# Routing joined, high and low parts gathered apart, expert weights with eight neighbouring features per partition

## The chip, the cores and the metric

The kernel runs on one core of one Trainium2 chip, alone. The metric is the device time of one execution in microseconds. TensorE (PE), VectorE (DVE), ScalarE (ACT), GpSimd (POOL) and SyncE (SP) run side by side, each through its own list of instructions, and wait for each other by semaphores.

## What is computed

Two layers of a decoder trunk on 256 tokens of 1024 features, all in float32. A layer is a mixer of three kinds of attention, a cross-attention into 256 memory tokens, and a grouped mixture of experts, each followed by a layer norm. The change is in the third part, `TOP_K` is 2, with four groups of four experts:

```python
scores = jax.nn.sigmoid(x @ router_w)                  # 16 experts
biased = scores + router_bias
grp = biased.reshape(B, S, 4, 4)
g_sel = jnp.argmax(jnp.sum(lax.top_k(grp, 2)[0], axis=-1), axis=-1)
masked = jnp.where(in_group[..., None], grp, NEG_INF).reshape(B, S, 16)
_, expert_idx = lax.top_k(masked, 2)
w = jnp.take_along_axis(scores, expert_idx, axis=-1)
w = w / jnp.sum(w, axis=-1, keepdims=True)             # gates of the two
a = jax.nn.silu(x @ w_gate[e]) * (x @ w_up[e]) * gate[e]
out = sum over e of a @ w_down[e]                      # x <- LayerNorm(alpha*x + out)
```

## The kernel before, in words

**Products in two parts.** Every large product runs in fp32r, with each operand split in a high and a low part. `product` (lines 1467 to 1471) makes three matmuls, high by high, high by low, low by high. ScalarE writes the high part of a weight (`split_hi`, a rounding copy), VectorE the low one (`split_lo`, a subtraction).

**The weight stream.** Weights come in sub-loads of up to 512 KB, in a fixed order, through a ring of 12 slots (`raw`). SP issues the load of sub i when the low part of sub i − 12 is made. There are four slots for split weights; ScalarE splits sub i when TensorE has used sub i − 4. N1 is the number of the first sub of the experts. An expert takes four subs for gate and up (each two chunks of 128 features, 256 gate columns and 256 up columns) and two for down.

**The order of the mixture part, in a layer.** Each engine's order is written out by hand.
- `x` is transposed to `xT`, features on partitions, in a high and a low part. TensorE forms the router product "RT" with the weights as the stationary side, 16 experts (and unused columns) by 256 tokens. ScalarE copies it to `logitT`, TensorE turns it back to tokens on partitions ("GT", lines 1851 to 1858), and ScalarE takes the exponential.
- VectorE works out the group of each token (`router_groups`, 1148 to 1177), step by step, each waiting for the one before. `first_best` marks the first maximum in a row, one operation per tile of 128 tokens. The group comes out as `ing`, a 0/1 table.
- Meanwhile ScalarE makes `xs_hi`, the high part of `x`, and GpSimd `xs_lo` (659 to 662).
- TensorE counts each token's place in its group with products by the tables `upto` and `ones` in fp32 (1677 to 1684), VectorE turns this to `posg` and to `sel`, a 0/1 table of tokens by 4 × 128 places.
- `gather`: for each of 8 chunks f of 128 features, four matmuls (high and low part, two tiles) add up in one bank of PSUM the features f*128 to f*128+127 of the tokens of all groups. ScalarE and VectorE copy the banks in turn to `xg`, in float32.
- For each group the token block is split to `cur_hi` and `cur_lo` (`cur_of`, lines 768 to 771 and 1231 to 1236), for group 0 at once, for the others between the splits of the group before, at its second expert.
- Experts in turn: `experts_up` (24 matmuls of 512 columns), `act_of`, `turn_a`, `experts_down` (12). `turn_sel` comes between the first two experts, `place_gates` in the middle of the second expert's up part. `router_first` and `router_gates` (1190 to 1223) work out the two experts and their gates; the end of `router_gates` finds whether a group has over 128 tokens and sets `flag`.
- `y_of` reads a group's result, `scatter` puts it back to the tokens.

## Time and profile before

| | us |
|---|---|
| median of 3 runs | 956.23 |
| the runs | 952.37, 956.23, 956.77 |
| the profiled execution | 951.58 |
| its span, first to last instruction | 950.0 |
| TensorE busy (matmul) | 835.7 (88%) |
| VectorE busy | 648.5 (68%) |
| ScalarE busy | 496.9 (52%) |
| GpSimd busy | 95.0 (10%) |

The span is the time between the first and last instruction, the rest of the profiled execution lies around it. Busy times are sums over the span; matmuls overlap, so two that follow each other at once show starts closer together than their durations. A matmul has two rows, its load of the stationary operand (PEld, LDWEIGHTS) and itself (PE, MATMUL). In the timeline, instructions of one line that follow each other are merged in one row ("x2"), and the bracket names the idle time of that engine before the row and who ended it. The mean granted TensorE clock is 0.946 of full.

### The profile page before, as it was taken

What the parts mean: (1) busy time and instruction counts of PE and PEld (TensorE: products, weight loads), DVE (VectorE), ACT (ScalarE), POOL (GpSimd) and SP (SyncE); (2) the same over time, 40 slices, a digit from 0 to 9 for tenths busy, and PEclk for the clock granted to TensorE, in tenths of its full rate; (3) what the DMA queues carried; (4) which work ended last, traced back from release to release, by engine and by line L of the source; (5) the groups of instructions that cost most, each with busy time, mean ns of one, the idle gap of its engine ahead of it and who ended that gap; (6) DMA issues with size and microseconds to landing.
All of it is one profiled execution on the core that took longest, in us unless ns stands there. A gap on an engine that the chain in (4) does not pass through costs nothing.

```text
span 950.0 us, 12092 instructions
## 1 busy us (share of the span) xinstructions
PE 835.7 (88%) x4292; PEld 701.7 (74%) x4292; DVE 648.5 (68%) x1137; ACT 496.9 (52%) x799; POOL 95.0 (10%) x169
## 2 busy tenths in 40 slices
PE   4989999989965899999689989999898489999994
PEld 4987887879854677777488878878886467777773
DVE  6456766574547798989555576577564667989983
ACT  4555544444333587877345554454443335878761
POOL 7122200020012000000121130002000200000001
PEclk9999999999977999999989999999999589999997
DMA  9842432653322599999364425344524227999931
GB/s 305 270 134 98 156 123 94 218 179 112 114 86 89 170 333 350 337 346 338 103 181 132 145 90 178 111 159 158 171 92 134 83 73 262 346 344 351 339 108 45
DMA packets 124094, 177.06 MB, mean 186 GB/s; under 512 B 12304, under 2 KB 92704, under 8 KB 124032
## 3 DMA queue, kind: packets, MB, share of 16 engines
q1 hardware_dynamic: 122048, 169.56, 53.7%
q0 software_dynamic: 1984, 6.70, 2.3%
q8 instruction: 36, 0.59, 0.3%
q14 instruction: 26, 0.21, 0.1%
HBM read 175.18 MB, written 1.05 MB: 186 GB/s over the span
## 4 chain that ended last, share of the span: by engine, by line
PE 75%; DVE 14%; ACT 4%; issue 3%; POOL 2%; ACTq 0%; DVEq 0%; POOLq 0%
PE bank L1469 20%; PE bank L1471 19%; PE bank L1470 19%; DVE w_lo L515 5%; PE bank L1692 2%; ACT w_hi L509 2%; PE bank L1619 2%; PE bank L1723 2%; PE bank L1599 2%; PE bank L1588 1%; PE bank L1577 1%; PE bank L1628 1%; PE bank L1566 1%; DVE xT_lo L1004 1%; PE bank L1576 1%
## 5 line engine op out<-in xcount | busy, mean ns | idle before, releaser
L515 DVE TENSOR_TENSOR w_lo<-raw,w_hi 128x1024 fp32r<-128x1024 f32 (+2 forms) x336 | 382.4, 1174 | 87.2 <-ACT w_hi L509 86.1
L509 ACT ACTIVATE w_hi<-raw 128x1024 fp32r<-128x1024 f32 (+2 forms) x336 | 326.2, 1007 | 121.7 <-PE bank L1471 121.1
L1469 PE MATMUL bank<-w_hi,cur_hi 128*128 128x512 f32 x256 | 104.5, 408 | 8.5 <-DVE w_lo L515 8.5
L1471 PE MATMUL bank<-w_hi,cur_lo 128*128 128x512 f32 x256 | 101.3, 396 | 0.0
L1470 PE MATMUL bank<-w_lo,cur_hi 128*128 128x512 f32 x256 | 101.0, 395 | 0.0
L1469 PE MATMUL bank<-w_hi,xT_hi 128*128 128x384 f32 (+1 forms) x224 | 79.2, 353 | 8.3 <-DVE xT_lo L1004 7.9
L1470 PE MATMUL bank<-w_lo,xT_hi 128*128 128x384 f32 (+1 forms) x224 | 76.8, 343 | 0.0
L1471 PE MATMUL bank<-w_hi,xT_lo 128*128 128x384 f32 (+1 forms) x224 | 76.7, 342 | 0.0
L614 POOL TENSOR_SCALAR st<-st 128x1 f32<-128x1 f32 x12 | 7.0, 581 | 678.2 <-ACT junk L760 677.7
L718 ACT ACTIVATE qkT<-bank 66x512 f32<-66x512 f32 (+2 forms) x32 | 19.0, 594 | 90.3 <-PE bank L1566 90.3
L1469 PEld LDWEIGHTS bank<-w_hi,cur_hi 128*128 128x128 f32 x256 | 48.7, 190 | 21.2 <-DVE w_lo L515 6.7
L1469 PE MATMUL bank<-w_hi,aT_hi 128*128 128x512 f32 x128 | 53.0, 414 | 8.3 <-DVE w_lo L515 6.0
L1471 PEld LDWEIGHTS bank<-w_hi,cur_lo 128*128 128x128 f32 x256 | 48.7, 190 | 10.6
L1470 PEld LDWEIGHTS bank<-w_lo,cur_hi 128*128 128x128 f32 x256 | 48.9, 191 | 9.1
L1469 PE MATMUL bank<-xT_hi,w_hi 128*128 128x256 f32 x144 | 45.3, 315 | 9.1 <-DVE xT_lo L1004 9.1
L1469 PE MATMUL bank<-w_hi,mixT_hi 128*128 128x512 f32 x128 | 51.0, 398 | 0.0
L1469 PEld LDWEIGHTS bank<-w_hi,xT_hi 128*128 128x128 f32 x224 | 43.0, 192 | 10.7 <-issue 9.2
L1471 PE MATMUL bank<-w_hi,aT_lo 128*128 128x512 f32 x128 | 50.8, 397 | 0.0
L1470 PE MATMUL bank<-w_lo,aT_hi 128*128 128x512 f32 x128 | 50.7, 396 | 0.0
L1470 PE MATMUL bank<-w_lo,mixT_hi 128*128 128x512 f32 x128 | 49.9, 390 | 0.0
L1471 PE MATMUL bank<-w_hi,mixT_lo 128*128 128x512 f32 x128 | 49.9, 390 | 0.0
L775 ACT ACTIVATE aT_hi<-bank 128x256 fp32r<-128x256 f32 x32 | 12.3, 384 | 63.3 <-PE bank L1648 63.3
(291 smaller groups left out, 1684.1 us busy)
## 6 DMA issues: line engine op xcount, KB each, us to landing
raw<-in_expert_w_gate_dram SPq DMA_DIRECT2D x128, 256.0 KB, 4.3
raw<-in_expert_w_up_dram SPq DMA_DIRECT2D x128, 256.0 KB, 5.0
raw<-in_expert_w_down_dram SPq DMA_DIRECT2D x64, 512.0 KB, 4.9
raw<-in_w_in_dram SPq DMA_DIRECT2D x48, 384.0 KB, 4.1
raw<-in_xattn_w_kv_dram SPq DMA_DIRECT2D x32, 512.0 KB, 3.5
raw<-in_w_mix_out_dram SPq DMA_DIRECT2D x16, 512.0 KB, 4.2
raw<-in_xattn_w_q_dram SPq DMA_DIRECT2D x16, 512.0 KB, 4.3
raw<-in_xattn_w_o_dram SPq DMA_DIRECT2D x16, 512.0 KB, 4.3
```

The costliest lines, as they stand in the source:

```text
L509: nc.scalar.activation(w_hi[:, split_slot(i, p), 0:w], raw[:, slot, 0:w], ACT.Copy).then_inc(hi_ready.sem, 1)
L515: nc.vector.tensor_tensor(w_lo[:, split_slot(i, p), 0:w], raw[:, slot, 0:w], w_hi[:, split_slot(i, p), 0:w].bitcast(F32), ALU.subtract).th ...
L718: nc.scalar.activation(qkT[0:d, h % 2, :], B_QK[0:d, :], ACT.Copy).then_inc(qkT_ready.sem, 1)
L775: nc.scalar.activation(aT_hi[:, par, :, :], bank[2 + par][:, 0:2 * P].rearrange("p (c t) -> p c t", c=2), ACT.Copy).then_inc(aT_a.sem, 1)
L1004: nc.vector.tensor_tensor(xT_lo[:, 4 * h:4 * h + 4, t * P:(t + 1) * P], b[:, :].rearrange("p (k m) -> p k m", k=4), hi.bitcast(F32), ALU.s ...
L1469: nc.tensor.matmul(o, lhs[0], rhs[0], start=first, stop=False, skip_group_check=shared)
L1470: nc.tensor.matmul(o, lhs[0], rhs[1], start=False, stop=False, skip_group_check=shared)
L1471: return nc.tensor.matmul(o, lhs[1], rhs[0], start=False, stop=last, skip_group_check=shared)
L1599: ins = nc.tensor.transpose(B_PT[:, k * P:(k + 1) * P], pr[:, k * P:(k + 1) * P], ident[:, :])
L1619: nc.tensor.matmul(o[:, 0:T], v[:, 0, g, :], pT[:, h % 2, 0:T], start=True, stop=False)
L1692: ins = nc.tensor.matmul(bank[XG_BANK[f]][:, :], v[:, t, f * P:(f + 1) * P], sel[:, t, :], start=n == 0, stop=n == 3)
L1723: ins = nc.tensor.matmul(bank[2 * t + h][:, :], selT[:, g, t * P:(t + 1) * P], v[:, g, 512 * h:512 * h + 512], start=g == 0 and v is y_hi, ...
```

## The change

Router: the product is turned over, the tokens are the stationary side and 16 expert columns are moved, so the logits come out with tokens on partitions. Routing works on both tiles in one operation each, with broadcast operands; the score of a group, the sum of its two largest, is found as the maximum of three kinds of pairs; the two experts of a token come from counting how many of the four in its group are ahead. `upto`, `ones` and `ing` become fp32r, and `xs_lo` is made by VectorE. The gather keeps the high and the low part in banks of their own and writes them as `xg_hi` and `xg_lo`, so `cur_of` is gone. Its stationary operand takes every eighth column, so partition p of chunk f holds feature 8p + f; the gate and up weights are read by the same rule, so that a sub brings rows 8p+2j and 8p+2j+1 to partition p. `full_group` is split off `router_gates` and comes after the first `act_of`. At the start of the kernel VectorE writes `ones`, `upto` and `earlier`, and TensorE waits for them. The tables `desc16` and `logitT` are gone; places in SBUF are moved.

```diff
+        XG_BANKS = ((6, 7), (2, 3), (0, 1))
+        LO_BY_ACT = (2, 5)
+        spread = lambda w: w.rearrange("(p k) n -> p k n", p=P)
...
-                    load(l, i + j, slot, [(r[:, :, g, :], feat(w[l][e])[:, 2 * j:2 * j + 2, :])
+                    load(l, i + j, slot, [(r[:, :, g, :], spread(w[l][e])[:, 2 * j:2 * j + 2, :])
                                           for g, w in enumerate((expert_w_gate, expert_w_up))])
...
-                for t in range(TT):
-                    pool.wait_ge(xs_a.sem, xs_a.at(l, t + 1))
-                    nc.gpsimd.tensor_tensor(xs_lo[:, t, :], xs[:, t, :], xs_hi[:, t, :].bitcast(F32), ALU.subtract)\
-                        .then_inc(xs_p.sem, 1)
...
-                wait_job(l, "RT")
-                nc.scalar.activation(logitT[0:NE, :], bank[2 * pair["RT"]][0:NE, 0:T], ACT.Copy).then_inc(job_a.sem, 1)
-                wait_job(l, "GT")
-                nc.scalar.activation(rt[:, 0, :], bank[2 * pair["GT"]][:, 0:TT * NE], ACT.Exp, scale=-1.0)\
                 for t in range(TT):
                     nc.scalar.activation(xs_hi[:, t, :], xs[:, t, :], ACT.Copy).then_inc(xs_a.sem, 1)
+                wait_job(l, "RT")
+                nc.scalar.activation(rt[:, 0, :], banks("RT")[0][:, 0:TT * NE], ACT.Exp, scale=-1.0)\
+                    .then_inc(job_a.sem, 1)
...
-                for f in range(0, KC, 2):
+                for f in range(KC):
                     act.wait_ge(xg_done.sem, xg_done.at(l, f + 1))
+                    for n, dst in ((0, xg_hi), (1, xg_lo)):
+                        if n == 0 or f in LO_BY_ACT:
+                            nc.scalar.activation(dst[:, f, :, :].rearrange("p g s -> p (g s)"),
+                                                 bank[XG_BANKS[f % 3][n]][:, :], ACT.Copy).then_inc(xg_a.sem, 1)
...
+            nc.vector.tensor_copy(ones[:, :], ones_f[:, :]).then_inc(fp_tables, 1)
+            nc.vector.tensor_copy(upto[:, :], upto_f[:, :]).then_inc(fp_tables, 1)
+            nc.vector.tensor_scalar(earlier[:, :, :], order[:, :, :], 0.5, None, ALU.is_gt).then_inc(fp_tables, 1)
...
+                step(nc.vector.tensor_scalar(R[1], R[0], 1.0, None, ALU.add))
+                step(nc.vector.reciprocal(R[2], R[1]))
+                step(nc.vector.tensor_tensor(by_tile(R[3], NE), by_tile(R[2], NE),
+                                             rbias[:, :].unsqueeze(1).to_broadcast([P, TT, NE]), ALU.add))
+                step(nc.vector.tensor_tensor(more, first, second, ALU.max))
+                step(nc.vector.tensor_tensor(both, first, second, ALU.add))
+                step(nc.vector.tensor_tensor(across, more[:, :, 0], more[:, :, 1], ALU.add))
+                step(nc.vector.tensor_tensor(within, both[:, :, 0], both[:, :, 1], ALU.max))
+                step(nc.vector.tensor_tensor(score, across, within, ALU.max))
+                step(nc.vector.tensor_reduce(best, by_tile(score, NG), AX, ALU.max))
+                step(nc.vector.tensor_tensor(cand, by_tile(score, NG), best.unsqueeze(2).to_broadcast([P, TT, NG]), ALU.is_equal))
+                step(nc.vector.tensor_tensor(G4(R[10]), G4(R[10]), desc4[:, :], ALU.mult))
+                step(nc.vector.tensor_reduce(ahead, cand, AX, ALU.max))
+                step(nc.vector.tensor_tensor(by_tile(ing_r[:, :], NG), cand, ahead.unsqueeze(2).to_broadcast([P, TT, NG]), ALU.is_equal))
...
...
...
                 turn_x(l, "XT1c", 1)
+                for t in range(TT):
+                    dve.wait_ge(xs_a.sem, xs_a.at(l, t + 1))
+                    nc.vector.tensor_tensor(xs_lo[:, t, :], xs[:, t, :], xs_hi[:, t, :].bitcast(F32), ALU.subtract)\
+                        .then_inc(xs_v.sem, 1)
                 for i in range(N1, N1 + 2):
                     split_lo(dve, l, i)
+                router_groups(l)
+                split_lo(dve, l, N1 + 2)
+                place_tokens(l)
+                for f in range(KC):
+                    if f not in LO_BY_ACT:
+                        dve.wait_ge(xg_done.sem, xg_done.at(l, f + 1))
+                        nc.vector.tensor_copy(xg_lo[:, f, :, :].rearrange("p g s -> p (g s)"),
+                                              bank[XG_BANKS[f % 3][1]][:, :]).then_inc(xg_v.sem, 1)
+                    if f == 1:
+                        split_lo(dve, l, N1 + 3)
+                    if f == 4:
+                        router_first(l)
                 split_lo(dve, l, N1 + 4)
-                router_gates(l, step)
                 split_lo(dve, l, N1 + 5)
+                router_gates(l)
                 dve.wait_ge(gs_done.sem, gs_done.at(l, 1))
...
                 act_of(l, 0, 0)
+                full_group(l)
                 for i in range(N1 + 6, N1 + 8):
...
-                        if j == 1:
-                            for h in range(2):
-                                cur_of(l, p + 1, h)
...
+            pe.wait_ge(fp_tables, 3)
             pe.wait_ge(mem_in, 16)
...
-                        lhs = tuple(v[:, kc, :] for v in (cur_hi, cur_lo))
+                        lhs = tuple(v[:, kc, e // EPG, :] for v in (xg_hi, xg_lo))
...
+                    for n, v in enumerate((xs_hi, xs_lo)):
+                        for t in range(TT):
+                            ins = nc.tensor.matmul(bank[XG_BANKS[f % 3][n]][:, :], v[:, t, f:DM:KC], sel[:, t, :],
+                                                   start=t == 0, stop=t == TT - 1)
...
+                routers = [sub_in(l, index["RT", j]) for j in range(2)]
                 for t in range(TT):
+                    for kc in range(KC):
+                        lhs = tuple(v[:, kc, t * P:(t + 1) * P] for v in xT)
+                        r = tuple(v[:, (kc % 4) * NE:(kc % 4 + 1) * NE] for v in routers[kc // 4])
+                        ins = product(banks("RT")[0][:, t * NE:(t + 1) * NE], lhs, r, t == 0 and kc == 0,
+                                      t == TT - 1 and kc == KC - 1, shared=True)
+                ins.then_inc(split_free.sem, 2)
                 gather(l)
-                experts_up(l, N1, 0, range(4), None, 0)
+                experts_up(l, 0, N1, range(4))
                 turn_sel(l)
```

## Rows read from the trace of the kernel before

**Rows 1.** The page, section 4: the chain by engine.
```profile
PE 75%; DVE 14%; ACT 4%; issue 3%; POOL 2%; ACTq 0%; DVEq 0%; POOLq 0%
```

**Rows 2.** Windows of layer 0: length, busy us (instructions), granted clock, DMA share, GB/s.
```profile
340.00:354.00 14.00, 13.40 (x59) 10.15 (x58) 12.49 (x15) 11.16 (x15) 0.00 (x0) 1.00 1.02 343
...
285.00:297.70 12.70, 2.27 (x10) 2.21 (x10) 9.42 (x25) 5.44 (x7) 5.78 (x4) 0.60 0.23 83
...
312.00:326.00 14.00, 10.56 (x51) 8.42 (x50) 9.52 (x24) 6.58 (x9) 0.00 (x0) 0.88 0.43 139
```

**Rows 3.** Timeline, product and routing: start us, duration us, instruction [idle <-releaser].
```profile
278.54 0.55 PE L1469 MATMUL bank<-xT_hi,w_hi 128*128 128x256 f32 x1 [2.27 <-DVE xT_lo L1004]
...
283.59 0.41 PE L1471 MATMUL bank<-xT_hi,w_lo 128*128 128x256 f32 x1
...
284.97 0.20 ACT L894 ACTIVATE rt<-bank 128x32 f32<-128x32 f32 x1 [0.56 <-PE bank L1855]
...
285.20 0.18 DVE L1158 TENSOR_SCALAR rt<-rt 128x32 f32<-128x32 f32 x1 [4.71 <-ACT rt L894]
...
285.42 0.35 DVE L1159 RECIPROCAL rt<-rt 128x32 f32<-128x32 f32 x1
...
286.19 4.67 POOL L661 TENSOR_TENSOR xs_lo<-xs,xs_hi 128x1024 fp32r<-128x1024 f32 x2 [14.06 <-ACT xs_hi L898]
...
286.22 2.34 DVE L1165 TENSOR_TENSOR rt<-rt 128x8 f32<-128x8 f32 x1
...
288.56 2.33 DVE L1167 TENSOR_TENSOR rt<-rt 128x8 f32<-128x8 f32 x1
...
292.69 0.16 DVE L1143 TENSOR_REDUCE rt<-rt 128x2 f32<-128x8 f32 x1
...
292.89 0.49 DVE L1145 TENSOR_SCALAR ing<-rt 128x4 f32<-128x4 f32 x2
```

**Rows 4.** Timeline, ranking, gather and the first expert, TensorE.
```profile
293.53 0.56 PE L1679 MATMUL bank<-ing,upto 128*128 128x4 f32 x2 [8.59 <-DVE ing L1145]
...
293.95 0.57 PE L1679 MATMUL bank<-ing,ones 128*128 128x4 f32 x2
...
297.75 0.77 PE L1692 MATMUL bank<-sel,xs_hi 128*128 128x512 f32 x1 [1.95 <-DVE sel L1184]
...
306.74 0.39 PE L1469 MATMUL bank<-w_hi,cur_hi 128*128 128x512 f32 x1
```

**Rows 5.** Loads of TensorE: two source lines (ns min/median/max) and a timeline row.
```profile
L1679 PEld LDWEIGHTS bank<-ing,upto x8: 288/333/338, 293.5 to 759.5; 128*128 128x128 f32 x8
...
L1692 PEld LDWEIGHTS bank<-sel,xs_hi x32: 187/188/338, 297.7 to 772.2; 128*128 128x128 f32 x32
...
317.84 1.98 PEld L1701 LDWEIGHTS bank<-g,sel 128*128 128x128 f32 x16
```

**Rows 6.** Timeline, first expert.
```profile
310.59 0.18 DVE L1203 SCALAR_TENSOR_TENSOR rt<-rt 128x32 f32<-128x32 f32 x1
...
315.31 1.21 DVE L515 TENSOR_TENSOR w_lo<-raw,w_hi 128x1024 fp32r<-128x1024 f32 x1
...
316.57 0.51 PE L1469 MATMUL bank<-w_hi,cur_hi 128*128 128x512 f32 x1 [1.96 <-DVE w_lo L515]
```

**Rows 7.** Timeline, `cur_lo` beside expert 2.
```profile
344.44 1.29 DVE L1235 TENSOR_TENSOR cur_lo<-xg,cur_hi 128x512 fp32r<-128x512 f32 x2
...
347.06 0.47 PE L1469 MATMUL bank<-w_hi,cur_hi 128*128 128x512 f32 x1 [0.55 <-DVE w_lo L515]
```

**Rows 8.** The page, section 6: pieces, KB each, us to landing.
```profile
raw<-in_expert_w_gate_dram SPq DMA_DIRECT2D x128, 256.0 KB, 4.3
...
raw<-in_xattn_w_kv_dram SPq DMA_DIRECT2D x32, 512.0 KB, 3.5
```

**Rows 9.** Timeline, start of the kernel.
```profile
8.29 3.32 PE L1460 MATMUL bank<-ident,mem_tok 128*128 128x128 f32 x16 [8.29 <-POOL offf L571]
...
8.35 1.08 DVE L986 TENSOR_SCALAR offs<-offs 128x256 int32<-128x256 int32 x2 [0.99 <-DMA rbias<-in_router_bias_dram]
```

More of the change, by code:

```diff
@@ L225, in build @@
         qTx, e4 = sb("qTx", [P, KC, T], at=q_work)
-        xg, m0 = sb("xg", [P, KC, NG, P], at=work)
-        cur_hi, m1 = sb("cur_hi", [P, KC, P], F32R, at=m0)
-        cur_lo, m2 = sb("cur_lo", [P, KC, P], F32R, at=m1)
+        xg_hi, m0 = sb("xg_hi", [P, KC, NG, P], F32R, at=work)
+        xg_lo, m2 = sb("xg_lo", [P, KC, NG, P], F32R, at=m0)
         y_hi, m3 = sb("y_hi", [P, NG, DM], F32R, at=m2)
@@ L1155, in step, with router_groups @@
                     dve.wait_ge(route.sem, route.at(l, q[0]))
[L1157 removed]
+                return step
+            def router_groups(l):
+                q[0] = 0
+                step = stepper(l)
+                dve.wait_ge(job_a.sem, job_a.at(l, evac_a[job["RT"]]))
                 step(nc.vector.tensor_scalar(R[1], R[0], 1.0, None, ALU.add))
                 step(nc.vector.reciprocal(R[2], R[1]))
[L1160 to L1162 removed]
@@ new lines, in router_groups @@
+                four = R[3].rearrange("p (g i) -> p g i", i=EPG)
+                first, second = four[:, :, 0:EPG:2], four[:, :, 1:EPG:2]
+                more, both = (R[i][:, 0:2 * TT * NG].rearrange("p (g i) -> p g i", i=2) for i in (4, 5))
+                step(nc.vector.tensor_tensor(more, first, second, ALU.max))
+                step(nc.vector.tensor_tensor(both, first, second, ALU.add))
+                across, within, score = (G4(R[i]) for i in (6, 7, 8))
+                step(nc.vector.tensor_tensor(across, more[:, :, 0], more[:, :, 1], ALU.add))
@@ L1430, in _ @@
                         expert_turn(l, p * EPG + (j + 1), (j + 1) % 2, 6 * j, p, p if j == EPG - 1 else None)
-                        if j == 1:
-                            for h in range(2):
-                                cur_of(l, p + 1, h)
                 for j in range(2):
@@ L1786, in _ @@
                     for s in range(t + 1):
-                        ins = nc.tensor.matmul(o, (ones if s < t else upto)[:, :], lf[:, s, :], start=s == 0, stop=s == t)
+                        ins = nc.tensor.matmul(o, (ones if s < t else upto)[:, :].bitcast(F32), lf[:, s, :],
+                                               start=s == 0, stop=s == t)
                 ins.then_inc(turned.sem, 1)
```

231 lines of the change are left out of this document (88 added, 143 removed), and 2 rows, old and new, of the table jobs.

## The prediction

> **What bounds the kernel now.** I read the chain that ended last first: 75% of it lies on TensorE, 14% on VectorE [rows 1]. So a microsecond counts only where TensorE waits, or where its own list of work gets longer or shorter. Then I read stretches of layer 0 [rows 2]. In the expert stage (340 to 354) TensorE is busy 13.40 of 14 us at the full clock, 59 matmuls or 0.23 us each, with the DMA engines at 1.02 and 343 GB/s. In the routing stretch (285 to 297.7) it is busy 2.27 of 12.70 us while VectorE is busy 9.42: there VectorE is the path, and there this change works. All of it happens twice; layer 1 repeats the pattern.
>
> The reader should see three things in the timeline. First, the last product matmul starts at 283.59, the first routing step at 285.20, and the last half of `ing` is written at about 293.4, so routing takes 8.2 us. In it two operations of 8 columns take 2.34 and 2.33 us, where their like take 0.16, just while GpSimd forms `xs_lo` (4.67 us for two) [rows 3]. Second, ranking, `sel` and gather follow one another, up to the first expert at 306.74 [rows 4]. Third, TensorE waits 1.96 us for a weight split that stands in VectorE's queue behind `router_gates` [rows 6].
>
> **The change, part by part, per layer.** Durations are of the one profiled execution.
>
> *Router product: a cost.* Now 24 matmuls move 256 columns each; from 278.54 to 283.59 are 23 intervals of 0.22 [rows 3], the low of TensorE's two levels (256 columns at 1.2 GHz are 0.21). After it there are 3 × 8 × 2 = 48 matmuls that move 16 columns, each with its own load of 128 columns, and the load is the price. The trace has no fp32r matmul of so few columns. The nearest rows: the ranking's fp32 passes of 4 columns, two of which begin 0.42 after the two before, 0.21 each at the low level [rows 4]; and the 16 loads of `place_gates` in 1.98, 0.12 each, at the high one [rows 5]. A load takes the same in both types (fp32 0.333 at the low level, the slowest fp32r one 0.338) [rows 5], so I take the same interval. The stretch begins after a wait of 2.27 and keeps the low level to its end [rows 3]. I take 48 × 0.213 = 10.2 against 5.1: +5.1. Bounds: +0.6, if it has the full clock at once (48 × 0.12 = 5.7), and +15, if a small fp32r matmul needs two passes as an fp32 one does (48 × 0.42 = 20).
>
> *Hop to routing: a gain.* The copy of `logitT`, the two transposes and their waits go. From the product's end (283.59 + 0.41) to 285.20 are 1.2; Exp (0.20) and two hand-overs stay, 0.3. −0.9 [rows 3].
>
> *Group routing: the gain.* `xs_lo` goes to VectorE, ahead of routing: two operations of about 1.2 like a weight split (1.21 [rows 6]), beside the product, which has its inputs already and is now 10 us long; the splits of N1 and N1+1 queue behind them (2.4), and on these only loads 12 sub-loads ahead wait. GpSimd then does nothing beside routing, so 2.34 and 2.33 become 0.2 each. The chain is 13 steps: 12 × 0.20, since a small step starts 0.20 after the one before (292.69, 292.89), and a reciprocal, 0.39 with its hand-over: 2.8 against 8.2. −5.4 [rows 3]. If another stall came in the place of GpSimd's, 4.3 of this would stay. What could be late next is split N1+2, queued between routing and `place_tokens` (1.2): ScalarE has its high half some 2.5 after Exp (function table, Silu, split), and VectorE would wait 1.3 for the ranking there anyway. I cost it at nothing, at 1.2 if that cover fails.
>
> *Ranking: a gain.* Five products in fp32 are ten passes, in fp32r five: −5 × 0.21 = −1.1 [rows 4]; 0 if fp32r of 4 columns takes two passes.
>
> *Gather: nothing, with a wide bound.* 32 matmuls before and after, 8.99 from the first to the expert's first, 0.28 each, partly at the low level [rows 4]. Their loads now take every eighth column. The trace has no such load; contiguous ones take 0.187 [rows 5] and can follow each other every 0.12. The moving side (512 columns, 0.23 at the high level [rows 2]) sets the pace, so there is no gain below nothing, and only a load of over 0.23 shows. No row bounds that above; I choose four times 0.12: 32 × (0.48 − 0.23) = +8. I take 0, since even twice the contiguous time hides. Ten evacuations on ScalarE and six plus a split on VectorE fit in some 8 us, with three pairs of banks in turn; as they write the high and low parts at once, `cur_hi` and `cur_lo` of group 0 go too.
>
> The Trainium skill speaks against this part. Its page "SBUF — State Buffer" (section "Door 1: The DMA port swizzle") says that reads want two hits in a line of 16 bytes and that each crossing to a new line pays a penalty; a step of eight fp32 columns has one hit per line. It gives no size for TensorE, and no row here shows one. By the rule the load gets longer, by how much is rival B.
>
> *First expert: a gain.* `router_gates` (from 310.59) stands before split N1+5 (315.31), and TensorE idles 1.96 [rows 6]. After the change the split comes first, ready about 5 us after the expert begins (two subs of 1.36 freed, ScalarE 1.0, VectorE 1.2); TensorE needs it after 24 × 0.23 and eight transposes, 6.5. The wait goes; the nine steps of `router_gates` (2) end before TensorE asks for `g4`. But `full_group` (four steps, 0.8) now stands behind `act_of` and ahead of split N1+6, for which TensorE waits already. −2.0 + 0.8 = −1.2.
>
> *Later groups: a gain.* `cur_lo` (two operations, 1.29) stands between splits and TensorE waits 0.55 behind it [rows 7], three times a layer. −1.6. The stalls behind `y_of` are not touched.
>
> *Weight loads: nothing.* Pieces stay 1 KB at the destination, 256 KB land in 4.3 us, and a slot comes round only after 12 sub-loads, some 17 us, so about 10 us of lateness is covered. Rows with a pitch of 8 KB are read already, `w_kv`, 512 KB in 3.5 [rows 8].
>
> *Start: a cost, once.* TensorE now also waits for three small VectorE operations behind `offs2`, which starts at 8.35 and takes 1.08; with 0.5 for the three TensorE begins at 10.0, not 8.29 [rows 9], and the way to the first product goes through these transposes. +1.7, between 0 (something later hides it) and 3.
>
> Sum per layer: 5.1 − 0.9 − 5.4 − 1.1 + 0 − 1.2 − 1.6 = −5.1; twice, and the start: −10.2 + 1.7 = −8.5. Against the profiled execution, 951.58 with a span of 950.0, that is 943.1. The median of the three runs is 4.65 above the profiled one; from it, 956.23 − 8.5 = 947.7. I forecast 947.5.
>
> **Rivals.** (A) The product gets the full clock, or its loads are cheaper than the fp32 rows say: +0.6 instead of +5.1, 9 less in all, 938.5. For it: it is twice as long and never pauses. Against it: 16 moved columns per load leave the array mostly idle, and in the stretch that holds `place_gates`, of the same kind, the granted clock is 0.88 over 312 to 326 although TensorE is busy for 10.56 of 14 [rows 2].
> (B) Slower: the strided load binds the gather. From 0.23 a load on every further 0.1 costs 3.2 per layer; from 0.36 on it eats the whole gain, and at 0.48 it is 16 for both: 963.5. This is what the skill's rule would do here. For it speaks only that no row shows a strided load; against it, that a contiguous load leaves half of the interval free.
> (C) Small fp32r matmuls need two passes: product +15, not +5, ranking no gain: 947.5 + 2 × 11 = 969.5.
> (D) The change does not do what it says: another stall, or split N1+2, keeps routing slow, 4 a layer: 955.5, no change.
>
> **How the numbers follow.** The forecast with its own small errors (±4) 0.55, A 0.18, B 0.12, C 0.05, D 0.10. Within 0.5% of 956.23, about what a measurement of this kernel can tell from no change, lies 951.4 to 961.0. Faster: A and nearly all of the forecast, 0.70. Slower: C and the upper end of B, 0.10. The rest of B, D and the forecast's upper end are no change, 0.20. The range leaves out C and the ends of A and B: 938 to 960.
>
> **What would show it.** Routing near 2.8 with no step over 0.4 in it; 48 loads 0.21 apart in the product (0.12 says A, 0.42 says C); loads of the gather near 0.19 (over 0.23 says B); no idle of 1.96 before the second expert, some 1.5 before its third sub; no idle of 0.55 in later groups; the first transpose at 10. The prediction is wrong if the product's loads have another price, or if loads set the pace of the gather.

## The result, and the profile after

The changed kernel takes 943.6 us (median of four runs, 942.97 to 944.69), the kernel before 956.48 on the same chip (952.37 to 956.77). The ratio is 0.988, 95% interval 0.985 to 0.991: faster, by 1.2%. The forecast was 947.5 in a range of 938 to 960. The two profiled executions are closer together, 951.58 and 944.16: 7.4 us, where 8.5 were worked out.

The chain of the page, by engine; before it was 75% and 14% [rows 1].

```profile
PE 82%; DVE 9%; ACT 3%; issue 3%; POOL 2%; DMA 1%; DVEq 0%; ACTq 0%; POOLq 0%
```

VectorE's share is 5 points smaller, TensorE's 7 larger: the routing became short, the router product long. The windows of layer 0 say the same (length, busy us with instructions in the order PE, PEld, DVE, ACT, POOL, granted clock, DMA share, GB/s).

```profile
273.00:282.00 9.00, 3.93 (x16) 3.13 (x16) 6.72 (x8) 4.01 (x8) 3.75 (x6) 0.51 0.22 73
282.00:292.60 10.60, 10.32 (x48) 10.31 (x48) 4.63 (x4) 1.02 (x2) 0.00 (x0) 0.50 0.45 137
292.60:299.00 6.40, 1.39 (x7) 1.28 (x6) 5.25 (x18) 3.58 (x5) 0.00 (x0) 0.50 0.15 44
299.00:304.00 5.00, 5.00 (x12) 4.03 (x13) 1.99 (x3) 1.19 (x2) 0.00 (x0) 0.51 0.12 50
304.00:309.00 5.00, 5.00 (x22) 4.96 (x22) 3.31 (x8) 3.75 (x7) 0.00 (x0) 1.00 0.30 105
```

The second row is the product: TensorE is busy for 10.32 of 10.60 us and the granted clock is 0.50, the lower level, throughout. It stays there until about 304, deep in the gather. GpSimd does nothing from 282 on.

The timeline of the same stretch answers to [rows 3, 4].

```profile
282.27 0.35 PE L1466 MATMUL bank<-w_hi,xT_hi 128*128 128x16 f32 x1 [2.27 <-DVE xT_lo L1001]
...
292.29 0.36 PE L1468 MATMUL bank<-w_hi,xT_lo 128*128 128x16 f32 x1
...
292.69 0.20 ACT L898 ACTIVATE rt<-bank 128x32 f32<-128x32 f32 x1 [9.67 <-PE bank L1468]
...
292.92 0.18 DVE L1153 TENSOR_SCALAR rt<-rt 128x32 f32<-128x32 f32 x1 [6.18 <-ACT rt L898]
...
295.56 0.17 DVE L1173 TENSOR_TENSOR ing<-rt 128x8 fp32r<-128x8 f32 x1
295.76 1.22 DVE L528 TENSOR_TENSOR w_lo<-raw,w_hi 128x1024 fp32r<-128x1024 f32 x1
...
295.78 0.37 PE L1677 MATMUL bank<-ing,upto 128*128 128x4 f32 x1 [3.13 <-DVE ing L1173]
...
298.89 1.21 PE L1691 MATMUL bank<-sel,xs_hi 128*128 128x512 f32 x2 [1.88 <-DVE sel L1183]
...
308.94 0.39 PE L1466 MATMUL bank<-w_hi,xg_hi 128*128 128x512 f32 x1
```

The 48 small matmuls start from 282.27 to 292.29, (292.29 − 282.27) / 47 = 0.213 apart, 10.2 us in all. Routing runs from 292.92 to 295.73, 2.8 us, with no step over 0.35. The gather takes 308.94 − 298.89 = 10.05 us, 8.99 before.

In the first expert, against [rows 6], the wait of 1.96 is gone. The over-full test (its last step at 321.29) stands ahead of the split that TensorE waits for:

```profile
320.78 0.53 PE L1647 MATMUL bank<-ident,act_a 128*128 128x128 f32 x2 [0.85 <-DVE act_a L1227]
...
321.29 0.16 DVE L1222 CAST flag<-fl 1x2 int32<-1x2 f32 x1
321.37 2.34 DVE L528 TENSOR_TENSOR w_lo<-raw,w_hi 128x1024 fp32r<-128x1024 f32 x2
...
322.63 0.79 PE L1466 MATMUL bank<-w_hi,xg_hi 128*128 128x512 f32 x1 [1.32 <-DVE w_lo L528]
```

At the start TensorE waits for the last of the three new conversions, and begins at 9.99 in place of 8.29 [rows 9]:

```profile
9.99 1.30 PE L1457 MATMUL bank<-ident,mem_tok 128*128 128x128 f32 x5 [9.99 <-DVE earlier L983]
```

The two spans are 950.0 and 942.4 us. Where the difference lies, from the starts of the rows that bound each stretch (us, after less before):

| stretch | layer 0 | layer 1 | worked out |
|---|---|---|---|
| start to the product of layer 0 | +3.73 | | +1.7 |
| end of layer 0 to the product of layer 1 | | −1.03 | 0 |
| product's start to the ranking | −1.48 | −1.16 | −1.2 |
| ranking to gather | −1.11 | −1.31 | −1.1 |
| gather | +1.06 | +0.17 | 0 |
| first expert to the transposes of the fifth | −1.27 | −1.09 | −1.7 |
| from there to the scatter | −1.32 | −2.82 | −1.1 |

The stretch from the scatter of layer 1 to the end is 20.8 us before and 20.9 after. The rows add up to −7.63, against −8.5 worked out. Two of them are in part chance of the two executions. In the last one of layer 1, 1.5 of the 2.82 lie in the down product of the last expert, 4.36 us before and 2.85 after: over 926 to 930 the granted clock of the kernel before was 0.59, while in the changed kernel it was 1.00 at this place (918 to 922). In layer 0 neither kernel has such a stretch there. The first, +3.73, is taken up again below.

### The profile page after: what moved, and what is told of

Same layout as the page of the kernel before. It is cut to its first block, busy times and chain, and to the rows that moved or that the text cites. A ratio compares the mean times of both kernels' runs of the same rounds, so it can differ in the third digit from the quotient of the medians.

```text
span 942.4 us, 12097 instructions
## 1 busy us (share of the span) xinstructions
PE 845.8 (90%) x4326; PEld 714.4 (76%) x4326; DVE 629.4 (67%) x1090; ACT 494.6 (52%) x793; POOL 85.6 (9%) x165
## 4 chain that ended last, share of the span: by engine, by line
PE 82%; DVE 9%; ACT 3%; issue 3%; POOL 2%; DMA 1%; DVEq 0%; ACTq 0%; POOLq 0%
PE bank L1466 22%; PE bank L1468 21%; PE bank L1467 21%; DVE w_lo L528 3%; PE bank L1691 2%; PE bank L1616 2%; PE bank L1720 2%; PE bank L1596 2%; PE bank L1585 2%; PE bank L1574 1%; PE bank L1625 1%; PE bank L1563 1%; DVE xT_lo L1001 1%; PE bank L1573 1%; ACT w_hi L522 1%
## 5 line engine op out<-in xcount | busy, mean ns | idle before, releaser
L1466 PE MATMUL bank<-w_hi,xg_hi 128*128 128x512 f32 x256 | 105.2, 411 | 2.7 <-DVE w_lo L528 2.7
L1468 PE MATMUL bank<-w_hi,xg_lo 128*128 128x512 f32 x256 | 102.0, 399 | 0.0
L1467 PE MATMUL bank<-w_lo,xg_hi 128*128 128x512 f32 x256 | 102.0, 399 | 0.0
L1466 PE MATMUL bank<-w_hi,xT_hi 128*128 128x384 f32 (+2 forms) x256 | 90.7, 354 | 12.1 <-DVE xT_lo L1001 11.7
L1468 PE MATMUL bank<-w_hi,xT_lo 128*128 128x384 f32 (+2 forms) x256 | 88.4, 345 | 0.0
L1467 PE MATMUL bank<-w_lo,xT_hi 128*128 128x384 f32 (+2 forms) x256 | 88.4, 345 | 0.0
L1468 PEld LDWEIGHTS bank<-w_hi,xg_lo 128*128 128x128 f32 x256 | 49.2, 192 | 11.3
L1467 PEld LDWEIGHTS bank<-w_lo,xg_hi 128*128 128x128 f32 x256 | 49.4, 193 | 9.2
L1467 PEld LDWEIGHTS bank<-w_lo,xT_hi 128*128 128x128 f32 x256 | 53.7, 210 | 0.3
L1468 PEld LDWEIGHTS bank<-w_hi,xT_lo 128*128 128x128 f32 x256 | 53.6, 209 | 0.2
```

The source lines that it names most:

```text
L1466: nc.tensor.matmul(o, lhs[0], rhs[0], start=first, stop=False, skip_group_check=shared)
L1467: nc.tensor.matmul(o, lhs[0], rhs[1], start=False, stop=False, skip_group_check=shared)
L1468: return nc.tensor.matmul(o, lhs[1], rhs[0], start=False, stop=last, skip_group_check=shared)
```

## The experiments

Each run is compared with the kernel before on its own chip; where it is set against the changed kernel, that is the first of the table. e0 to e2b ran on one chip, e3 to e6 on a second, e7 to e9 on a third, e10 on a fourth. The medians of the kernel before were 953.83, 954.61, 953.00 and 953.52 there, so a difference of about 1 us between runs of different chips says nothing by itself.

| kernel | median us | ratio to before | interval |
|---|---|---|---|
| e0_after | 944.03 | 0.990 | 0.988 to 0.993 |
| e1_product_back | 934.29 | 0.981 | 0.978 to 0.983 |
| e2a_pool_early | 944.70 | 0.992 | 0.989 to 0.994 |
| e2b_pool_late | 952.08 | 0.998 | 0.996 to 1.000 |
| e3_contiguous | 943.65 | 0.989 | 0.986 to 0.993 |
| e4_one_cur | 947.00 | 0.992 | 0.990 to 0.995 |
| e5_casts_late | 942.72 | 0.988 | 0.984 to 0.991 |
| e6_full_later | 943.49 | 0.989 | 0.986 to 0.993 |
| e7_all | 931.55 | 0.978 | 0.973 to 0.982 |
| e8_filled | 937.05 | 0.984 | 0.980 to 0.988 |
| e9_all_filled | 920.26 | 0.965 | 0.961 to 0.969 |
| e10_more_filled | 917.25 | 0.961 | 0.958 to 0.964 |

### The changed kernel again

> The changed kernel once more, beside the three variants below on the same chip, so that differences of a few us can be read. Every theory expects 943 to 945 us (its first runs: 943.0 to 944.7), and in the trace the router product of layer 0 in 48 matmuls 0.21 us apart and 10.2 us long.

944.03 us (943.08 to 944.49), the product from 282.36 to 292.38. The kernel before had a median of 953.83 here. So the change is worth 10 to 13 us by medians (9.8 here, 12.9 in the first comparison).

### The router product alone in its old form

```
-  routers = [sub_in(l, index["RT", j]) for j in range(2)]
-  for t in range(TT): for kc in range(KC): ...   # tokens stationary, 16 columns moved
+  lhs = tuple(v[:, k * NE:k * NE + P] for v in parts)
+  ins = product(banks("RT")[0][:, 0:T], lhs, tuple(v[:, kc, :] for v in xT), ...)
...
+  nc.tensor.transpose(banks("GT")[0][:, t * NE:(t + 1) * NE], logitT[0:NE, t * P:(t + 1) * P], ...)
```

> The changed kernel with the router product alone put back in its old form: 24 matmuls of 256 columns, the copy of the logits, the two small transposes and a third hop before the exponential. Theory of the prediction (the new product is 5.1 us a layer dearer than the old one at the low clock, the hop that goes with it 0.9 cheaper): this kernel is 4.2 us a layer faster than the changed kernel, 8.4 together, 935 to 936 us. Theory that the small matmuls also keep the granted clock low for longer (in the changed kernel it returns at 303.9 us, during the gather; in the kernel before it returned at 301.3): the gather is faster too, by up to 1.5 us a layer, and the whole 932 to 934 us. Rival: xs_lo and the split of the routers' weights stand on VectorE beside the product, so a shorter product only waits for them: less than 3 us gained in all, 941 us or more, and the trace then shows TensorE idle behind VectorE ahead of the ranking matmuls.

934.29 us: 9.7 faster than the changed kernel. Its timeline of layer 0:

```profile
280.65 0.55 PE L1469 MATMUL bank<-xT_hi,w_hi 128*128 128x256 f32 x1 [2.27 <-DVE xT_lo L1004]
...
285.70 0.35 PE L1471 MATMUL bank<-xT_hi,w_lo 128*128 128x256 f32 x1
...
290.19 0.34 PE L1680 MATMUL bank<-ing,upto 128*128 128x4 f32 x1 [3.22 <-DVE ing L1176]
...
293.27 1.22 PE L1694 MATMUL bank<-sel,xs_hi 128*128 128x512 f32 x2 [1.88 <-DVE sel L1186]
...
303.84 0.40 PE L1469 MATMUL bank<-w_hi,xg_hi 128*128 128x512 f32 x1
```

From the product's start to the ranking are 9.54 us, with the straight product 295.78 − 282.27 = 13.51: 4.0 less, the −4.2 of the theory. In layer 1 it is 13.51 against 9.61, 3.9, and the gather there is 9.15 in place of 10.35, since the clock is back sooner (at about 753.5, 3 us after the gather's start; in the changed kernel at about 764.5, over 5 us after it). In layer 0 the gather is no shorter: 10.57 in place of 10.05, with the granted clock at 0.50 over its first 6 us. The rival fell, nothing stood behind VectorE. The first theory holds for 7.9 of the 9.7 us. The second came true in one layer of two, and its gain is not steady. The profiled executions differ by 10.7 us, of which 1.6 lie ahead of the product of layer 0, where the two kernels are the same. So the part of the change that does away with the turning back is a loss of about 8 us, hidden under the gain of the others.

One number of this timeline is worth a look: 24 matmuls of 256 moved columns begin (285.70 − 280.65) / 23 = 0.220 apart, the first interval being long and the others 0.21, and those of 16 columns 0.213 apart. **At the lower level a matmul of 16 columns costs TensorE as much as one of 256.**

### What made the routing short: the place of `xs_lo`, or its engine

In e2a_pool_early, GpSimd forms `xs_lo` again, at the new early time; in e2b_pool_late moreover ScalarE makes `xs_hi` behind the exponential, as before the change.

```
-  dve: nc.vector.tensor_tensor(xs_lo[:, t, :], xs[:, t, :], xs_hi[:, t, :].bitcast(F32), ALU.subtract)
+  pool: nc.gpsimd.tensor_tensor(xs_lo[:, t, :], xs[:, t, :], xs_hi[:, t, :].bitcast(F32), ALU.subtract)
e2b only: the two copies to xs_hi moved from ahead of wait_job(l, "RT") to behind the exponential
```

> The changed kernel with xs_lo computed on GpSimd again (two subtractions of 4.7 us), but begun at the new early place of xs_hi, so that it runs beside the router product and ends before or with the routing's first steps. Theory (the saving in the routing came from where this work stands in time, beside the product, and not from the engine that does it): within 1.5 us of the changed kernel, 942 to 946 us. Since the second subtraction ends about 292 us after the start, at most the routing's first step should be touched. Rival (it is the engine: GpSimd's subtraction and VectorE's work beside it slow each other wherever they meet): the splits of the routers' weights on VectorE are late, the product starts later, and the whole is 4 us or more slower, 948 us or more.

> The changed kernel with xs_hi copied after the exponential, as before the change, and xs_lo on GpSimd behind it, beside the new routing of 13 steps. Theory (before the change two waits of 2.3 us stood in the routing because VectorE had to wait while GpSimd subtracted; they are worth 4.3 us a layer and come back with the overlap): 8 to 9 us slower than the changed kernel, 951 to 953 us, with two routing steps of over 2 us in the trace in place of 0.2 us. Rival (the steps themselves were what the old routing cost, the overlap was incidental): the 13 steps stay at 0.2 us each, the only cost is that xs_lo is later for the gather, and the whole is within 3 us of the changed kernel.

e2a 944.70 us, the same as the changed kernel; e2b 952.08, 8.1 slower. The rows of e2a, GpSimd and the VectorE split beside it:

```profile
280.34 6.55 POOL L674 TENSOR_TENSOR xs_lo<-xs,xs_hi 128x1024 fp32r<-128x1024 f32 x2 [6.28 <-ACT xs_hi L900]
...
280.07 4.56 DVE L528 TENSOR_TENSOR w_lo<-raw,w_hi 128x1024 fp32r<-128x1024 f32 x2
```

And of e2b:

```profile
294.69 4.67 POOL L674 TENSOR_TENSOR xs_lo<-xs,xs_hi 128x1024 fp32r<-128x1024 f32 x2 [18.03 <-ACT xs_hi L904]
...
294.74 2.34 DVE L1167 TENSOR_TENSOR rt<-rt 128x16 f32<-128x16 f32 x1
297.11 2.27 DVE L1169 TENSOR_TENSOR rt<-rt 128x8 f32<-128x8 f32 x1
```

Where two long operations meet, both are slowed: two splits take 4.56 in place of 2.35, GpSimd 6.55 in place of 4.67. Where GpSimd meets the small steps, it takes 4.67 as before the change, and two steps are held: an operation of 16 columns takes 2.34 and one of 8 columns 2.27, in place of 0.17. In e2a the meeting lies beside the product and costs nothing; in e2b it lies in a chain of steps and costs 2.34 + 2.27 − 2 × 0.17 = 4.3 a layer, 8.5 for both, measured 8.1. So 4.3 of the 5.4 us that the new routing gains are from moving one piece of work in time, and 1.1 from its fewer steps.

### Neighbouring columns

```
-  spread(w[l][e])            -  v[:, t, f:DM:KC]
+  feat(w[l][e])              +  v[:, t, f * P:(f + 1) * P]
```

> The changed kernel with the features in their old order: the gather loads 128 neighbouring columns instead of every eighth, and the experts' gate and up weights come as before with one feature row in each partition and piece. The result is the same. Theory (a strided load costs TensorE 0.017 us a matmul more than a neighbouring one at the high clock and nothing at the low one, and the DMAs are far from being awaited): 0.3 to 0.5 us a layer, 0.6 to 1.0 us together, 942.5 to 943.5 us; the gather's matmuls 0.2275 us apart at the high clock, its loads about 188 ns in place of 334 ns. Rival (the new order of the weights is what made the DMAs land later, 4.9 us a gate transfer in place of 4.3, and this is felt in the experts, where the changed kernel's chain shows DMA with 1% of the span): 3 to 5 us faster. A third possibility, that the long descriptors of the new order are a gain which the gather pays for: slower by 1 to 3 us, 945 to 947 us.

943.65 us, no difference that can be measured. The loads of the gather in all layers (ns min/median/max), of the changed kernel:

```profile
L1691 PEld LDWEIGHTS bank<-sel,xs_lo x32: 316/333/338, 299.5 to 768.9; 128*128 128x128 f32 x32
```

and of e3_contiguous:

```profile
L1691 PEld LDWEIGHTS bank<-sel,xs_lo x32: 187/188/330, 301.7 to 771.6; 128*128 128x128 f32 x32
```

The two levels of the clock have to be kept apart here. At the lower one both kinds take nearly the same, 0.336 us strided and 0.330 contiguous; at the higher one a strided load still takes 0.316 to 0.338, a contiguous one 0.187 to 0.188. The loads overlap, though: at the higher level 14 intervals between matmuls of the gather fill 305.04 to 308.47 in the changed kernel, 0.245 each, and 307.65 to 310.83 in this one, 0.227 each. That is 0.018 a matmul, for the some 20 that run at this level 0.4 us a layer. The rival, that the order of the weights makes their DMAs land later and that this is felt, is half right. In the six profiled kernels with the old order (the one before, e3, e4, e7, e9 and e10) the median gate transfer lands after 4.3 to 4.4 us, in the eight with the new order after 4.6 to 4.9, and the up transfers after 5.0 to 5.5 and 5.5 to 5.9. So the new order does make them land later, by some 0.3 us. It is not felt: 943.65 us here against 944.03, where the rival wanted 3 to 5 less.

### The split of the later groups left out

```
-  for h in range(2): cur_of(l, p + 1, h)      # on ScalarE and on VectorE, with TensorE's waits
```

> The kernel before the change with the split of the gathered tokens left out for groups 1 to 3 (experts of those groups work on group 0's tokens, so that part of the computation is not done). Theory (this split on VectorE stood in the way of the experts' weights and cost 1.6 us a layer, three stalls of 0.55 us at the groups' joints): 3.3 us faster than the kernel before, ratio 0.9965. From the groups' period in the two traces, 36.56 us before and 35.88 after, the gain would be 0.68 us for each of three groups, 2.0 a layer and 4.1 together, ratio 0.9957. Rival (the experts' time is set by TensorE or the DMAs and this stall only moves): within 1 us of the kernel before, ratio 0.999 or more, and another stall of the same size at the joints.

In this run the experts of groups 1 to 3 work on the tokens of group 0; the amount of work of TensorE is the same. 947.00 us, 7.6 below the median of before on its chip, more than either number; by profiled spans (950.0 and 945.9) it is 4.1. From the transposes of the fifth expert to those of the ninth are 358.60 to 395.17 = 36.57 in the kernel before, 360.03 to 395.81 = 35.78 here, and 35.87 in the changed kernel. So the joint of each group gives 0.7 to 0.8, not only the idle 0.55 of [rows 7]. The mechanism stands, with 2.1 to 2.4 a layer in place of 1.6. What the profile doesn't show is where the rest of the 7.6 comes from: in the first expert of layer 0, which this edit does not touch, it is even slower, since the granted clock is low longer (windows of before, then of e4_one_cur):

```profile
318.00:328.00 10.00, 8.52 (x39) 6.96 (x39) 7.17 (x9) 4.79 (x7) 0.00 (x0) 0.83 0.62 190
```

```profile
318.00:328.00 10.00, 8.77 (x30) 7.31 (x29) 6.10 (x8) 3.33 (x4) 0.00 (x0) 0.50 0.45 139
```

### The conversions at the start, and the over-full test

```
e5:  the three operations counted by fp_tables moved behind the memT_lo loop;
     pe.wait_ge(fp_tables, 3) moved from the start to the job "LT" of layer 0
e6:  full_group(l) moved behind split_lo(dve, l, N1 + 6) and split_lo(dve, l, N1 + 7)
```

> The changed kernel with the three conversions on VectorE at the start (the tables ones, upto and earlier) moved behind the subtractions that the first product needs, and TensorE's wait for them moved to the first use of these tables. Theory (TensorE starts 1.7 us late because of them, and everything behind is late by as much): 1.7 us faster than the changed kernel, 941.5 to 942.5 us, first transposes at 8.3 us after the start. The changed kernel was 3.4 us late by 58 us of layer 0; if the second half of this is from the same cause (the clock's low stretches lie elsewhere): 3.4 us faster, 940 to 941 us. Rival (the first product waits for its weights anyway): no difference, 943 to 945 us, with TensorE idle behind a DMA before the first product.

> The changed kernel with the four small steps that tell whether a group is over-full put behind the next two weight splits on VectorE instead of ahead of them. Theory (in the first expert TensorE waits 1.32 us for the low half of a weight split that stands behind these four steps, 0.65 us long): 0.6 to 0.8 us a layer, 1.2 to 1.6 together, 942 to 943 us, with that idle time at 0.6 us. Rival (VectorE is behind in any case and the next split or the low half of the activations is late by as much): within 0.4 us of the changed kernel, the idle time reappearing one step later.

e5 is at 942.72 us, 1.3 below the changed kernel, e6 at 943.49, 0.5 below it. A row of e5 and one of e6:

```profile
8.23 2.15 PE L1456 MATMUL bank<-ident,mem_tok 128*128 128x128 f32 x9 [8.23 <-POOL offf L584]
```

```profile
320.67 0.80 PE L1466 MATMUL bank<-w_hi,xg_hi 128*128 128x512 f32 x1 [0.70 <-DVE w_lo L528]
```

TensorE begins 1.76 earlier in e5, the first product at 18.80 in place of 20.11, so 1.3 of 1.7 arrive. In e6 the idle time is 0.70 as before the change, 0.6 less than in the changed kernel. Both did what was expected in the trace. Their medians are from another chip than the changed kernel's, and differences of 1.3 and 0.5 us are at the limit of what such times can tell; the gains rest on the traces.

### Four edits together, and TensorE kept at work

e7_all joins e1, e3, e5 and e6. e8_filled is the changed kernel with matmuls in TensorE's idle times whose result nobody reads; e9_all_filled has both.

```
+  def keep_busy(n_):
+      for _ in range(n_):
+          nc.tensor.matmul(bank[5][:, :], memT_hi[:, 0, 0:P], memT_hi[:, 0:2, :], start=True, stop=True)
...
+  keep_busy(18); turn_x(l, "XT0c", 0, 3); keep_busy(1); turn_x(l, "XT1c", 1, 4); keep_busy(8)
...
+  keep_busy(11)    # ahead of the wait for ing
...
+  keep_busy(6)     # ahead of the wait for sel
```

> The changed kernel with four of the single edits at once: the router product in its old form, the old order of the features, the conversions at the start moved back, and the over-full test behind two weight splits. If the gains are independent they add: from 944.0 us, 9.7 for the product (measured), 1.3 for the start, about 1.2 for the over-full test, about 0.7 for the loads: 931 us. Rival (they overlap, since each only removes cover of the next): 934 us or more, no better than the product alone.

> The changed kernel (straight product of 48 matmuls of 16 columns) with matmuls of 128x512 on tables that are there anyway, whose results nobody reads, put into the idle times of TensorE around the routing: 18 ahead of the first transposes (5.2 us idle), 1 between the two, 8 ahead of the product (2.3 us), 11 behind it (3.1 us), 6 ahead of the gather (1.9 us); sized by 0.23 us each at the high clock. Theory (the product costs 0.213 us a matmul because the granted clock is at its lower level, and it is there because TensorE idles around it; at the higher level 16 small matmuls took 1.84 us at the placing of the gates, 0.107 apart): the clock stays high, the product takes 5.1 us in place of 10.2, the gather 7.8 in place of 10.1, the transposes and ranking 1 us less: 8.4 us a layer, 927 us. Rival (small matmuls or the work around them bring the lower level whatever TensorE does in between): the clock falls all the same, the added matmuls take 0.43 us each, outlast the waits that they stand in, and cost 5.9 us a layer: 956 us.

> The four edits of e7_all with the same added matmuls as e8_filled. Theory of the clock: the old product takes 2.6 us in place of 5.1, the gather 7.3 in place of 9.2 to 10.6, transposes and ranking 1 us less, some 6 us a layer: 931 less 12, 919 us, and this form of the product stays ahead of the straight one by some 4 us (half of what it was) when both run at the high clock. Rival (the clock falls all the same): slower than e7_all by up to 12 us, 943 us. Rival (the added matmuls keep the clock high but hold up the vector engines' results by lying in TensorE's queue): gain under 4 us a layer, 923 us or more.

e7 931.55 us, 12.5 below the changed kernel, where the theory wanted 13: the four gains add. e8 937.05, between its two theories; its windows around the product:

```profile
274.00:279.70 5.70, 4.14 (x25) 3.15 (x25) 4.90 (x7) 3.26 (x6) 1.37 (x3) 1.00 0.19 78
279.70:282.60 2.90, 2.84 (x26) 2.87 (x26) 2.90 (x3) 0.81 (x1) 0.00 (x0) 1.00 0.60 215
282.60:287.30 4.70, 4.70 (x24) 4.70 (x23) 1.63 (x2) 0.00 (x0) 0.00 (x0) 0.50 0.48 140
287.30:292.90 5.60, 5.60 (x17) 4.54 (x17) 3.63 (x14) 3.58 (x5) 0.00 (x0) 0.50 0.22 74
```

With TensorE busy ahead of it, the product begins at the higher level: 26 matmuls in 2.90 us, 0.11 each. Then the granted clock falls in the middle of the product, though TensorE was busy for 2.84 of those 2.90 us, and the rest goes at 0.21. Layer 1 does the same: 0.11 apart from 737.49 to 740.09, then 0.21. The added matmuls behind it ran at the lower level too, 11 in 5.0 us, and outlasted the routing: `ing` was written at 290.6, the ranking began at 292.22. So the product took 7.6 us in place of 10.2, not 5.1. The whole is still 7.0 us below the changed kernel, so filling the idle times helps a stretch of small matmuls in part: at its start and in the gather behind it, not to its end.

The windows of e9, the old product and the gather:

```profile
280.80:283.90 3.10, 3.07 (x24) 2.87 (x24) 3.10 (x3) 0.74 (x1) 0.00 (x0) 1.00 0.58 186
...
291.00:298.40 7.40, 7.40 (x33) 6.10 (x34) 5.26 (x10) 4.96 (x9) 0.00 (x0) 1.00 0.35 125
```

The same fill, the same busy share, but 256 moved columns each: the clock stays high, the product takes 2.9 us (from 280.80 to 283.60), the gather 7.4, and the whole is 920.26 us, 11.3 below e7 and within 1.3 of the theory. The theories had put the two filled kernels 8 us apart (927 and 919), and they are 16.8 apart: under the fill the old form of the product keeps the clock, the straight one loses it. e8 and e9 also differ by the other three edits of e7, but those lie outside this stretch. It is 3.5% faster than the kernel before and 2.5% faster than the changed one.

The last run adds fill at the other idle places.

```
+  keep_busy(22), keep_busy(1), keep_busy(10)   # around the first transposes of layer 1
+  keep_busy(8)                                 # behind turn_x(l, "XT1b", 1, 2)
+  keep_busy(3, 3), keep_busy(2, 3)             # around turn_a of the first expert
```

> e9_all_filled with further matmuls whose results nobody reads, in the other idle times of TensorE behind which its trace shows the low level: 22, 1 and 10 at the start of the second layer (6.4, 0.6 and 3.0 us idle), 8 behind the transposes of the second norm (2.3 us), and 3 and 2 around the transposes of the first expert's activations (0.85 and 0.70 us). Theory (idle time brings the lower level, at whichever place): the low stretches of e9_all_filled at 208.3, 310.7, 460.9 to 474.5, 658.8 and 761.2 us go, together 27 us, of which TensorE worked some 17; at the high level that work takes half, so 8 us less, 912 us. Rival (in the first expert it is the 16 small matmuls that place the gates, as the small product did in e8_filled, and not the idle time around them): the stretches at 310.7 and 761.2 stay and the other ones go, 5 us less, 915 us. Rival (the added matmuls lie ahead of work that is ready): 918 us or more.

917.25 us, 3.0 below e9 on another chip, and nearest to the last rival's 918 or more. The mean granted clock rose from 0.975 to 0.985, so the theory was right on the clock and wrong on its worth: of the places it named, those at 208.3, 310.7, 658.8 and 761.2 are gone, at the start of layer 1 3.5 us of the low level are left (464 to 467.5), and a new low stretch stands at 723.5 to 727. First, e9_all_filled in the first expert, then e10_more_filled in the same place:

```profile
311.00:318.00 7.00, 6.65 (x17) 5.20 (x18) 5.71 (x10) 4.09 (x6) 0.00 (x0) 0.54 0.74 228
```

```profile
306.00:311.00 5.00, 4.96 (x31) 3.87 (x29) 1.49 (x3) 2.52 (x6) 0.00 (x0) 1.00 0.30 104
311.00:318.00 7.00, 6.39 (x27) 4.91 (x27) 6.83 (x12) 5.59 (x8) 0.00 (x0) 1.00 0.70 221
```

The rival on `place_gates` fell: its 16 small matmuls (307.52 to 309.36 in both) are there as before, and with the idle times around them filled the clock stays up. Between the two profiles lie 4.1 us: from the first expert to the scatter 2.3 in layer 0 and 0.9 in layer 1, from the scatter of layer 0 to the product of layer 1 0.9. Why no more came of it is not shown. In those 7 us TensorE gets through 27 matmuls (2 of them added) in place of 17 and is busy for 6.39, so it waits little; VectorE is busy for 6.83, so it may be the next limit, but no run tests that.

## Why the prediction was right, point by point

**The sign and the size.** Forecast 947.5, measured 943.6. The sum was −8.5, and the profiled executions differ by 7.4, the medians by 12.9 in the first comparison and 9.8 in the second. The prediction subtracted a difference between profiles from a median: over the comparisons the kernel before ran from 947.8 us, at a mean granted clock of 0.951, to 957.6 at 0.935, and the eight executions of the changed kernel stayed within 942.97 to 944.69. The profiled execution of before, at 0.946, lay in the faster half of this spread, the changed kernel's in the middle of its own. So by medians the change is worth more than one pair of profiles shows; why the kernel before varies so much more is open. That the sum came within 1 us of the profiles is in part luck. The terms of the router product, the routing and the ranking were right one by one; the start, the gather and the first expert were too favourable by 2.0, 1.2 and 1.4 us in all, the later groups gained 0.8 more than worked out, and 2.5 us came from two places for which the sum had nothing (1.5 in the last expert and 1.0 between the layers).

**Router product, +5.1.** Right to a tenth: 48 × 0.213 = 10.2, the first term of the sum, from the interval of the fp32 ranking passes. Rival A (it gets the full clock) had 0.18 and did not come; e8 shows that it would not have come with TensorE busy ahead of the product either, since the clock fell in its middle. The row brought against A does not bear on it: near `place_gates` the clock falls with the idle times around those matmuls, and in e10, where these are filled, it stays at 1.00. Rival C fell, one pass each. The turning back with its hop was sized at 0.9: e1 gives 4.0 net for both, worked out 4.2.

**Routing, −5.4.** Right: 2.8 us in 13 steps. The step that named GpSimd's work as the cause of the two long steps is shown by e2b. Rival D did not come. Split N1+2 lies beside the ranking as worked out (295.76 to 296.98, the ranking's last matmul ends at about 297.0) and costs nothing.

**Ranking, −1.1.** Right: 3.11 from its start to the gather, 4.22 before. No run changes this part alone; the reading rests on five intervals in place of ten.

**Gather, 0.** The rule of the Trainium skill on the page "SBUF — State Buffer" (section "Door 1: The DMA port swizzle") that each crossing to a new line of 16 bytes costs something holds here in kind: at the higher clock level a load with a step of eight takes 0.333 us where a contiguous one takes 0.188. At the lower level there is hardly a difference, 0.336 against 0.330. Rival B had the mechanism and not the size: at 0.33 a load the sum's own argument (only over 0.23 shows) would give 32 × 0.1 = 3.2 a layer, but the loads overlap and the interval rose from 0.227 to 0.245 only. That is 0.4 a layer at most; the rest of the +1.06 in layer 0 is the clock, at 0.51 over the first 5 us of the gather.

**First expert, −1.2.** −1.3 and −1.1 measured, over the part that holds one of the later joints too, where −1.7 were worked out. With 0.7 for the joint that leaves some −0.5 for the first expert, less than half of the term. The stall of 1.96 went, the over-full test costs 0.6 as e6 shows (1.32 against 0.70 idle); the granted clock of 0.66 over 318 to 328, 0.83 before, took part of the rest.

**Later groups, −1.6.** Mechanism right, the term too small: a joint gives 0.7 to 0.8 (e4 and the changed kernel alike), so 2.1 to 2.4 a layer. I had counted only the idle time of TensorE behind the one split.

**Weight loads, 0.** Right in the time. The landing itself was not left as it was: the gate transfers land later with the new order, 4.6 to 4.9 us in place of 4.3 to 4.4. As worked out, that much is covered (e3).

**Start, +1.7.** The first product was 1.7 late, and e5 brings 1.3 of it back. By the product of layer 0 it was 3.7. Here the second part was not foreseen. A granted clock of 0.57 in this window of the changed kernel stands against 1.00 before (the changed kernel, then the one before):

```profile
51.00:55.00 4.00, 3.63 (x12) 3.66 (x13) 1.02 (x4) 0.00 (x0) 0.00 (x0) 0.57 0.37 98
```

```profile
51.00:55.00 4.00, 4.00 (x23) 3.74 (x23) 1.48 (x3) 3.09 (x6) 2.17 (x4) 1.00 0.35 102
```

The conversions are not its cause: e5 has them moved away and has this low stretch (from 50 to 53.5), e6 keeps them and has not. Nor is it fixed to a kernel: e1, e3 and e6 are the same as the changed kernel up to the product of layer 0 (e3 but for the order of weights not yet used), and it begins at 280.65, 284.51 and 280.67 in them, at 282.27 in the changed kernel. These starts lie 3.9 us apart, so the 2 us beyond the 1.7 are within what differs between executions of the same instructions. What decides it stays open.

**What the prediction did not see** is that the largest single cost of the kernel around here was the lower level of the clock itself, from 273 to 304 in layer 0 and from 734 to 764 in layer 1. It took this as given. e9 shows that it was worth 11 us, as much as the whole change.

## What to carry to other kernels

Price a matmul with few moved columns by the interval at which such matmuls with a load each follow one another, not by its columns: 16 cost as much as 256 here, so turning a product over to save a transpose pays only if the number of matmuls doesn't rise. In a chain of small dependent steps look at what GpSimd does beside it before shortening the chain; moving that work in time was 4.3 of 5.4 us. And where TensorE idles a few us at a time and its clock is at the lower level, fill the waits with matmuls of full width that end before the wait does: 1.2 to 1.5% in this kernel. A stretch of 48 small matmuls lost the higher level after 2.8 us all the same, and a fill that outlasts its wait delays what stands behind it (1.6 us here).

## What the hardware showed that I had not expected

- A run of matmuls with 16 moved columns brings the granted clock down from 1.00 to 0.50 (2.4 to 1.2 GHz) while TensorE is busy for 2.84 of 2.90 us (e8, in both layers); the same stretch with 256 columns keeps 1.00 (e9).
- The interval of small matmuls is tied to the clock: 0.213 us at 1.2 GHz, 0.11 at 2.4, the same as for 256 columns (0.21 and 0.12).
- A load with a step of eight fp32 columns takes 0.333 us against 0.188 at the higher clock level and nearly the same as a contiguous one at the lower (0.336 and 0.330), and a run of them beside matmuls of 512 columns costs 0.018 a matmul only.
- Transfers of expert weights land some 0.3 us later when a partition takes two rows that follow each other in the matrix than when it takes two that lie 128 rows apart (4.6 to 4.9 us against 4.3 to 4.4, eight and six kernels).
- Long operations of GpSimd and VectorE that meet are both slowed: 6.55 in place of 4.67, and 4.56 in place of 2.35.
